# Building the gate table: first factor token by token on VectorE, second factor turned by GpSimd

## The reference, cut to what matters

```python
    expert = i1 * PEER_NKEYS + i2
    gate = jax.nn.softmax(best, axis=-1)
    ...
        u_sel = u_emb[ec]
        act = jax.nn.gelu(jnp.einsum('td,thkd->thk', tc, u_sel).astype(jnp.float32), approximate=False)
        return jnp.einsum('thk,thkd->td', (act * gc).astype(tc.dtype), v_emb[ec])
```

## Time and profile before

| what | value |
|---|---|
| median of three runs | 3759.49 us (3753.37 to 3774.87) |
| the profiled execution | 3772.18 us, span 3770.4 us |
| `spread_gates`, first comparison (1387.44) to last copy's end (1672.30) | 284.9 us |
| the same per group of 8 tokens, in steady state | 3.5 us, 80 groups |
| VectorE busy over the whole span | 2324.8 us (62%) |
| GpSimd busy over the whole span | 977.4 us (26%), nothing inside this stage |

### The profile page before, as it was taken

How to read it: one execution, slowest core, us unless ns; L and a number is a source line. 1 busy time by engine, 2 the same in 40 slices (tenths; PEclk the granted TensorE clock), 3 DMA queues, 4 the chain that set the end, 5 groups by cost and what they waited for, 6 DMA issues and landing times. The chain is left out here.

```text
span 3770.4 us, 47531 instructions
## 1 busy us (share of the span) xinstructions
PE 3248.3 (86%) x17309; PEld 2553.0 (68%) x17309; DVE 2324.8 (62%) x5058; ACT 942.6 (25%) x1346; POOL 977.4 (26%) x941
## 2 busy tenths in 40 slices
PE   8997998889676625546999999999999999999995
PEld 4444666664455515536999988888788888888883
DVE  2122334433499999974888877777777777544443
ACT  2212233331111115642222222222122222222221
POOL 0000000000023220001333345555555555222222
PEclk9996578989888869987999999999999999999998
DMA  4113101100200003557777779999999999666655
GB/s 183 47 59 92 25 17 34 45 17 34 94 26 26 13 1 101 167 162 261 252 246 258 247 270 349 351 354 355 346 346 351 351 351 353 243 227 219 219 208 195
DMA packets 326829, 706.22 MB, mean 187 GB/s; under 512 B 72432, under 2 KB 165872, under 8 KB 325104
## 3 DMA queue, kind: packets, MB, share of 16 engines
q0 software_dynamic: 110592, 402.70, 29.5%
q1 hardware_dynamic: 211328, 295.76, 22.6%
q10 hardware_dynamic: 4720, 5.26, 0.4%
HBM read 632.86 MB, written 70.78 MB: 187 GB/s over the span
## 5 line engine op out<-in xcount | busy, mean ns | idle before, releaser
L1548 PE MATMUL psum<-hn_hi_e,u_hi 128*128 128x320 f32 x2048 | 635.1, 310 | 59.1 <-DMA hn_lo_e<-scr_lo 55.5
L1548 PE MATMUL psum<-hn_hi_e,u_lo 128*128 128x320 f32 x2048 | 635.3, 310 | 0.0
L1548 PE MATMUL psum<-hn_lo_e,u_hi 128*128 128x320 f32 x2048 | 635.3, 310 | 0.0
L1532 POOL DMA_INDIRECT v_ring<-v_rows,eidT x384 | 440.7, 1148 | 699.4 <-PE psum L1591 593.4
L1564 PE MATMUL psum<-v_hi,w_hi 128*128 128x512 f32 x1280 | 511.6, 400 | 10.7 <-DVE coefT L1721 8.8
L1698 DVE TENSOR_TENSOR res<-psum,res 128x512 f32<-128x512 f32 x640 | 434.1, 688 | 124.4 <-PE psum L1564 124.4
L1564 PE MATMUL psum<-v_lo,w_hi 128*128 128x512 f32 x1280 | 501.5, 392 | 0.0
L1564 PE MATMUL psum<-v_hi,w_lo 128*128 128x512 f32 x1280 | 500.0, 391 | 0.0
L1525 POOL DMA_INDIRECT res<-u_rows,eid x288 | 339.7, 1179 | 387.4 <-DVE dots L1709 326.8
L1548 PEld LDWEIGHTS psum<-hn_hi_e,u_hi 128*128 128x128 f32 x2048 | 386.8, 189 | 64.7 <-DMA hn_lo_e<-scr_lo 55.7
L1678 DVE TENSOR_TENSOR w<-psum,w 128x640 f32<-128x640 f32 x128 | 105.6, 825 | 482.4 <-ACT psum L1631 482.4
(11 more groups left out here) (226 smaller groups left out, 4770.1 us busy)
## 6 DMA issues: line engine op xcount, KB each, us to landing
u_raw<-uT SPq DMA_DIRECT2D x128, 512.0 KB, 5.7
v_raw<-v_rows SPq DMA_DIRECT2D x128, 512.0 KB, 6.9
scr_g<-gates SPq DMA_DIRECT2D x5, 8192.0 KB, 30.6
w<-scr_g SPq DMA_DIRECT2D x128, 320.0 KB, 4.5
scr_m<-st_m SPq DMA_DIRECT2D x8, 1024.0 KB, 3.8
w_raw<-in_w_pq SPq DMA_DIRECT2D x8, 1024.0 KB, 5.5
w_in<-in_w_in SPq DMA_DIRECT2D x3, 2048.0 KB, 15.5
scr_a<-st_a SPq DMA_DIRECT2D x8, 768.0 KB, 3.2
```

Source lines behind the costliest of these rows:

```text
L1532: pool.indirect_dma_start(v_ring[:, m % V_RING, :], None, core.i["v_rows"], bass.IndirectOffsetOnAxis(eidT[:, m // P, t:t + 1], 0)).then_i ...
L1548: last = nc.tensor.matmul(ps[:, a, 0:COLS], x[:, c, j, :], y[:, j, a * COLS:(a + 1) * COLS], start=m == 0, stop=m == len(terms) - 1)
```

## The change: what it does

`one1` is gone. The first factor is made straight from the f32 number line, one instruction per token with two per-partition scalars (the slot's key and the slot's gate): compare, then multiply. The second factor's comparison stays, and its turn and widening move, for all 8 tokens in one instruction, from VectorE and ScalarE to GpSimd.

```diff
@@ spread_gates, VectorE
-                need(dve, second_act, n - BUFS + 1)
-                need(dve, first_ready, n - BUFS + 1)
-                need(dve, second_dve, n - BUFS + 1)
-                for z, dst in ((0, one1), (1, one2)):
-                    nc.vector.tensor_tensor(
-                        dst[:, b, :, :], iota[:, :, :],
-                        keysT[:, z, n * OCT:(n + 1) * OCT].rearrange("p (o t) -> p o t", o=1)
-                        .to_broadcast([P, NKEY, OCT]), ALU.is_equal).then_inc(ones_ready, 1)
+                need(dve, second_ready, n - BUFS + 1)
+                nc.vector.tensor_tensor(
+                    one2[:, b, :, :], iota[:, :, :],
+                    keysT[:, n * OCT:(n + 1) * OCT].rearrange("p (o t) -> p o t", o=1)
+                    .to_broadcast([P, NKEY, OCT]), ALU.is_equal).then_inc(ones_ready, 1)
                 need(dve, spread_done, n - BUFS + 1)
-                dve.wait_ge(ones_ready, n * 2 + 1)
-                nc.vector.tensor_tensor(
-                    first[:, b, :, :].rearrange("p t i -> p i t"), one1[:, b, :, :],
-                    flat[:, 2, n * OCT:(n + 1) * OCT].rearrange("p (o t) -> p o t", o=1)
-                    .to_broadcast([P, NKEY, OCT]), ALU.mult).then_inc(first_ready, 1)
-                dve.wait_ge(ones_ready, n * 2 + 2)
-                nc.vector.tensor_copy(second[:, b, ON_ACT:, :], one2[:, b, :, ON_ACT:].rearrange("p i t -> p t i")
-                                      ).then_inc(second_dve, 1)
+                for t in range(OCT):
+                    at = n * OCT + t
+                    nc.vector.tensor_scalar(first[:, b, t, :], iota_f[:, :], flat[:, 0, at:at + 1], flat[:, 2, at:at + 1],
+                                            ALU.is_equal, ALU.mult).then_inc(first_ready, 1)
+
+        @block.gpsimd
+        def _(pool):
+            for n in range(NOCT):
+                b = n % BUFS
+                pool.wait_ge(ones_ready, n + 1)
+                need(pool, spread_done, n - BUFS + 1)
+                nc.gpsimd.tensor_copy(second[:, b, :, :], one2[:, b, :, :].rearrange("p i t -> p t i")
+                                      ).then_inc(second_ready, 1)
@@ TensorE
-                pe.wait_ge(first_ready, n + 1)
-                pe.wait_ge(second_act, n + 1)
-                pe.wait_ge(second_dve, n + 1)
+                pe.wait_ge(first_ready, (n + 1) * OCT)
+                pe.wait_ge(second_ready, n + 1)
@@ ScalarE: widen(n) is removed, copy_out(n) stays
-            widen(0)
             for n in range(NOCT):
-                if n + 1 < NOCT:
-                    widen(n + 1)
                 copy_out(n)
```

More of the change, by code:

```diff
@@ L1273, in spread_gates @@
     NOCT = TD // OCT
-    ON_ACT = 4
     with ExitStack() as ctx:
@@ L1277, in spread_gates @@
         gates = [sb(f"gates{k}", [P, NKEY, P]) for k in range(2)]
-        one1 = sb("one1", [P, BUFS, NKEY, OCT], bf16)
         one2 = sb("one2", [P, BUFS, NKEY, OCT], bf16)
@@ L1283, in spread_gates @@
         iota = sb("iota_gb", [P, NKEY, OCT], bf16)
-        keysT = sb("slot_keys", [P, 2, TD], bf16)
+        keysT = sb("slot_keys", [P, TD], bf16)
         iota_in = sem("iota_in_g")
         iota_ready, keys_ready = sem("iota_ready_g"), sem("keys_ready_g")
-        ones_ready, first_ready, second_act, second_dve = (sem(x) for x in (
-            "ones_ready", "first_ready", "second_act", "second_dve"))
+        ones_ready, first_ready, second_ready = sem("ones_ready"), sem("first_ready"), sem("second_ready")
         spread_done, gates_out = sem("spread_done"), sem("gates_out")
@@ L1312, in _ @@
                                   .to_broadcast([P, NKEY, OCT])).then_inc(iota_ready, 1)
-            nc.vector.tensor_copy(keysT[:, :, :], flat[:, 0:2, :]).then_inc(keys_ready, 1)
+            nc.vector.tensor_copy(keysT[:, :], flat[:, 1, :]).then_inc(keys_ready, 1)
             dve.wait_ge(iota_ready, 1)
@@ L1350, in _ @@
         def _(act):
[L1351 to L1356, removed]
             def copy_out(n):
```

## The result

The changed kernel took 3829.5 us (median of ten runs, 3804.9 to 3874.9) beside 3764.9 us of the kernel before on the same chip (median of 25); four runs timed earlier gave 3826.0 beside 3759.8. The changed kernel takes 1.0163 times as long, 95% interval 1.0117 to 1.0209, which is 61 us (44 to 79). The prediction said 3815 us in 3720 to 3890. The rows here are from the second profile of the changed kernel (a run of 3813.5 us, span 3811.7); the first was of the 3871 us, and inside the stage both show the same group.

A forecast was written before the change was run, and what follows sets the result against it. VectorE's queue in the gate-table stage was taken as the bound, 3.50 us a group. With exclusion, 0.60 + 1.76 + 1.94 - 0.13 = 4.17 us, 54 us more over 80 groups: 3815 us, range 3720 to 3890.

The forecast's parts named there:

- The signs it named: Gate-table stage: comparisons 4.17 us apart, one tensor_scalar of eight some 2 us, others 0.28 to 0.34, TensorE idling about 2.1.
- Exclusion: Gate-table groups: double-rate tensor_scalars and two-input VectorE operations cannot run beside GpSimd's copy, so both queues add to 4.17 us.
- VectorE alone: VectorE's queue per group, if nothing else counted: 2.36 us instead of 3.50, saving 91 us over 80 groups.
- the upper bound: First factor's tensor_scalars: a second scalar costs as much as the first, 0.26 us each, 2.08 for eight.
- The sum's 1.94 for the copy: GpSimd's copy of 1024 elements per group, put at 1.94 us from ScalarE's turn, which has the same access.
- What hides: Per group: 0.13 us off for the held instruction's start already done; GpSimd's fixed 0.19 lies under VectorE's running instruction.
- The memset's 0.85 us: Low bound for GpSimd's copy of 1024 elements, from its memset at 0.83 ns an element.
- No exclusion: Rival: tensor_scalars run beside GpSimd's copy, a group takes 2.4 to 2.9 us, 48 to 91 us faster; chance 14%.
- The cheap copy: Rival: GpSimd's copy costs little more than its memset, 0.85 us; group 3.08, 34 us faster, 3726 us; chance 20%.
- the turning point: GpSimd copy of 1.27 us, where the group under exclusion equals the 3.50 us of before.
- The dear copy: Rival: the step costs GpSimd extra on its slower rate, copy 2.84 us; group 5.07, 126 us slower, 3885; chance 19%.

The follow-up runs named there:

- straight copy: Changed kernel with GpSimd's copy reading and writing 1024 neighbouring elements, the second factor's turn left out; group 3.37 us, stage 307.7 us.
- first factor alone: Kernel before, with only the first factor made by eight tensor_scalars, the turn staying on VectorE and ScalarE; stage 293.3 us, ratio 0.9943.
- number line in PSUM: Changed kernel with the eight tensor_scalars reading the number line from PSUM, three PSUM buffers instead of four; stage 290.4 us, ratio 0.9931.
- half the copy: Changed kernel with only tokens 4 to 7 turned by GpSimd and tokens 0 to 3 by ScalarE; group 3.47 us, stage 315.7 us.
- one scalar: Changed kernel with the constant 1.0 in place of the gate in each of the eight operations; group 3.95 us, stage 353.7 us.

## Why the prediction was right

*What bounds the kernel.* Right: VectorE's queue before and after, with the rest of the program only shifted by the stage's growth (2064.7 and 2064.3 us behind it). The signs it named came out too: one tensor_scalar of some 2 us among eight, and the others short.

*Exclusion.* This was argued from a two-input operation of 48 columns that lasted 2.39 us beside GpSimd, and carried over to a tensor_scalar that had no row. It is now shown: held to 2065 ns under a copy of 2.07 us, to 1170 under one of 1.19, to 1060 under one of 1.09, and never over 410 ns when the same operation reads PSUM. The Trainium skill, SBUF — State Buffer, section Who interferes with whom, gives this for the double-rate tensor_scalar; the trace agrees (335 ns against 2065), and the rows from PSUM agree with its other half, that an operation with at most one SBUF input outside that mode is left alone. From PSUM an operation costs 0.064 us more (0.32 against 0.256), near the 0.07 that the prediction gave for losing the double rate; so the experiment took away the SBUF read and, as it seems, the double rate together. Whether the same operation from SBUF at single rate would also go free wasn't tried; that a reduction and a reciprocal did speaks for it. Nor is it known whether it is the second read or the second write that is taken.

*The two halves of the change.* The prediction put VectorE alone at 91 us saved and let GpSimd take it back. The halves, run apart, are -26.5 us and +97.6 us, 71.1 together against 68.8 for the whole. The first half still has VectorE turning four tokens (0.53 us a group), so it is not all that VectorE is relieved of: one comparison and eight tensor_scalars are 0.60 + 2.05 = 2.65 us as measured, an estimate of 68 us for 80 groups where the prediction had 91.

*The sizes.* The forecast of a group was 4.17, measured 4.36; of the stage 54 us more, measured 68.8. One term is behind the miss. The tensor_scalar with two scalars costs 0.256, not 0.22: eight of them are 0.29 more. It was taken near the row with one scalar; the upper bound, that the second costs as much as the first, was the truth. The other two terms came out close, and both a little too long. The sum's 1.94 for the copy stands without GpSimd's fixed 0.19, which was to lie under VectorE's work; the whole copy was thus put at 2.13 and took 2.07, 0.06 less. What hides was put at 0.13 + 0.19 = 0.32 and is 0.37: not the start of a held instruction, but two of the eight (0.51) less the 0.14 by which the copy starts late. One finishes as the copy begins, one waits through it and ends with it. 0.29 - 0.06 - 0.05 = 0.18 of the 0.19. That the copy came out so near owes something to luck. It was taken from ScalarE's row, at 1.89 ns an element and 0.19 us fixed; the copies of 512 and 1024 elements (1.19 and 2.07 us) make it about 1.72 ns and 0.31 us, an estimate from two sizes. The memset's 0.85 us would have been wrong by more than half.

*TensorE.* It was to idle 2.1 us a group. It idled 139.7 us before 80 bursts, 1.75 us a group, still let go by `first`, because its clock fell and its bursts got longer.

*The rivals.* No exclusion is refuted by the held operations. The cheap copy is refuted by 2.07 us, though a copy without the step would have been one: 1.09 us is below the 1.27 at which the prediction put the turning point, and that run's group of 3.37 is indeed under 3.50. The dear copy (2.84) is refuted too. On the copy, the Trainium skill, GPSIMD Engine Reference, section 4.1 (Engine selection), is borne out by the straight copy alone: 1.09 us for 1024 elements, near ScalarE's 1.05. The Trainium skill, GPSIMD Engine Reference, section 7 (Performance pitfalls for Q7 kernels), has the direction right and not the size: the copy took 2.07 us where 2.5 was estimated from it, and the step added 0.98 us to 1.09, nearly double, where the section's figures differ by half.

## What to carry to other kernels

Work moved to GpSimd is not moved off VectorE's path if VectorE's instructions beside it are held by it: here those with two SBUF inputs and the tensor_scalars that read SBUF. The sign is a group of VectorE instructions with a short median whose longest is as long as GpSimd's instruction. Either let the VectorE operations beside GpSimd's work read PSUM (stage 290.4 us), or give the work to ScalarE, if it has room (275.0 us). A mean that no instruction has (549 between 335 and 2065) is worth a second look, and a change of two parts should be priced as two: here one part gained 26.5 us and the other lost 97.6.

## What the runs showed that was not expected

TensorE's granted clock in the stage fell from 1.00 to 0.80 with the change. Rows of the changed kernel, which answer to the earlier trace rows:

```profile
1400.00:1500.00 100.00, 60.36 (x367) 55.17 (x367) 100.00 (x207) 23.54 (x23) 47.74 (x23) 0.81 0.30 85
1500.00:1600.00 100.00, 61.30 (x368) 55.92 (x367) 100.00 (x208) 23.54 (x23) 47.72 (x23) 0.80 0.55 157
```

In a group of 4.36 us TensorE has 2.3 us to wait ahead of a burst that takes 2.05 us at the 2.4 GHz level. In the kernels where it waited 1.1 to 1.5 us a group (before, first factor alone, number line in PSUM, straight copy, half the copy) the granted clock was 1.00 from 1500 to 1600 us; with 1.9 us (one scalar) it was 0.86. With the clock moving between the 2.4 GHz level and the 1.2 GHz one, the same 16 records took 2.05 to 3.8 us. It cost nothing, since the group is longer than the slowest burst, but busy time (61.30 of 100 against 57.81) rose although TensorE did less: from its busy share alone one would read the opposite.
